# A one-core layer of RWKV-7 and differential attention: the triangle solve by rows down to nine columns, its results stored lane by lane, the x norm placed otherwise, K and V loaded by heads

## The chip, the cores and the metric

The kernel runs on one core of a Trainium2 chip. The metric is the device time of one execution in microseconds (us). Lower is better. Everything is in float32.

## The reference, cut to what matters

One layer is applied to two sequences, one of 512 and one of 2048 tokens (d_model 1024), which the kernel lays one behind the other as 2560 tokens.

```python
u = rmsnorm(h, norm_pre);  proj = u @ w_in
c = centred_conv(proj[..., :1728], conv_w, conv_b)          # r, k, v and three LoRA inputs
# RWKV-7 mixer, 8 heads of 64, in both directions of time; per direction and head:
#   sa    = state @ a_t
#   state = state * w_t + sa b_t^T + v_t k_t^T
#   y_t   = state @ r_t
y_rw = (groupnorm(y_fwd + y_bwd) + bonus) * silu(gate0)
# differential attention, 4 heads, q and k normed, ALiBi slopes:
att  = softmax(s0) - lam * softmax(s1);  o = rmsnorm(att @ v)
y_da = o * silu(gate1)
h = h + concat(y_rw, y_da) @ w_out
out = h + sigmoid(h @ ple_gate_w + b) * rmsnorm(p @ ple_proj)
```

The recurrence of a chunk of 128 tokens is turned into products of matrices. For that a unit lower (or upper) triangular matrix of 64 x 64 has to be inverted for each half of a chunk, each of 8 heads and both directions.

## The kernel before, in words

The work runs in stages, each a `Phase` with tiles and semaphores of its own. A barrier of all engines stands at the end of each, so nothing of one stage lies beside the next. Between stages the data goes through scratch tensors in DRAM. Engines run orders that are written out by hand, and a wait on an engine holds everything behind it on that engine. SP issues nearly all transfers, in program order. In order of time:

1. `conv_phase` (tiles named cv). The rmsnorm of x, the projection to the 1728 convolved columns, the convolution, decays, and the packing of operands for the later stages. There are NT = 20 chunks of 128 tokens, NB = 5 blocks of 512 and NK = 20 units k (a block b and a group g of 128 columns, G = 4). Chunks 0 to 3 are normed at the start. Chunk k + 4 is normed inside unit k: ACT squares (`x_square`, L278) and takes the root (`x_root`, L282), DVE scales the tile (`x_scale`, L403 and L405), TensorE transposes four columns of tiles at a time (`x_turn`, L547), and DVE evicts each such group (`x_evict`, L415). TensorE's own work of a unit is three columns of 32 matmuls (`column`, L561), small products, and the corner blocks of the triangle problem (`corners`, L607). The turn of 1/|kk| is `norms_turn` (L568). On DVE a unit goes: `norm` (L444, L447), `scans` (L453 to L464), `x_scale`, taps (L423, L425), `pack` (L479 to L486), `x_evict` (L415), more taps, and `var` (L440). POOL multiplies the packed operands (L268) beside it. On SP the loads of weights for k and v (L189) stand ahead of the loads of chunks 2 to 4 (L193), and `load(c)` waits until chunk c - 2 has been turned.
2. `rest_phase` (rs). TensorE projects 20 tiles of 128 tokens onto q, k, v and two gates (five units of 16 matmuls of 128 x 512 a tile, L903; four PSUM banks) and turns q and k (L885). ACT evicts and applies tanh, DVE does the norm of q and k (L845 to L854) and the gates (L859). Beside that DVE solves the triangles. For each block of 512 tokens (NJ = 5) the problem of each (direction, head half, group, chunk, half chunk) lies in a lane of its own: `al` holds A, `tt` becomes the inverse, both 64 x 64 a lane. Column k takes two instructions over m x n elements, m = k + 1 and n = 63 - k: a product into `tmp` (L833) and an add into `tt` (L835), each behind the one before. For m <= n, that is up to k = 31, the inner loop runs along a row of n neighbouring elements (the row form). From k = 32 it runs over the m elements of a column of `tt`, 64 elements apart (the column form). A planner (`costs`, `ends`) cuts the 63 columns into 12 slices of about equal cost, and a tile of tokens takes three slices. When a block is solved, ACT writes its transpose into `al` (L789), and SP stores both: 32 transfers a block, each of eight lanes in pieces of 256 bytes (L730, L731). In SP's order they stand behind the stores of a finished tile (L713, L716, L721) and ahead of those of the next. The block's `stored` count also lets `al` be loaded (L709) and `tt` be cleared (L763) two blocks later. The small loads of the identity and the five gain vectors (L738, L740) come behind u, the first weights and A, and both TensorE and DVE wait for them.
3. `unit_phase` (un). 80 units of matrix products. Each loads 5 pieces with SP (L964 to L968), two units ahead.
4. `chain_phase` (ch). Carries the states through the chunks.
5. `attention_phase` (at), once for each sequence (4, then 16 blocks of queries). All of K and all of V are loaded with one transfer each (L1386, L1387) into one semaphore `kv`, and TensorE waits for both before its first scores (L1525). DVE reduces the scores (L1478) with a table of distances that ACT copies (L1415).
6. `output_phase` (fn). The output projection and the gated residual.

## Time and profile before

| | us |
|---|---|
| three timed runs | 4258.77, 4259.48, 4265.96 |
| their median | 4259.48 |
| the profiled execution | 4262.29 |
| its span, first to last instruction | 4260.6 |
| TensorE busy in the span | 3633.9 (85%) |
| VectorE busy | 2541.4 (60%) |
| ScalarE busy | 1433.4 (34%) |
| GpSimd busy | 432.1 (10%) |
| mean granted TensorE clock | 0.932 |
| data moved | 406 MB, 95 GB/s on average |

The busy time of an engine is summed over all stages, which have different limits, so a share of the whole span says little. The profiled execution lies 2.81 us above the median of the timed runs, and 1.7 us of it lie outside its span. DMA shares are the mean over the core's 16 DMA engines. [...]

### The profile page before, as it was taken

How to read it: one execution, taken by the hardware profiler on the slowest of the kernel's cores; microseconds unless marked ns; L12 is line 12 of the kernel's file. 1: busy time of each engine (PE TensorE's matmuls, PEld its weight loads, DVE VectorE, ACT ScalarE, POOL GpSimd, SP SyncE). 2: the span in 40 equal slices, each digit the busy share in tenths (PEclk: the TensorE clock that was granted, in tenths of full speed). 3: DMA queues.
4: the chain of work that ended last, by engine and by line, in shares of the span. 5: the costliest groups of instructions: out<-in, count | busy, mean ns of one | idle time of the engine just before them, and what ended most of it. 6: DMA issues, size and time to landing. Idle time of an engine off the chain costs nothing. (4 is left out here: it accounts for less than half of the span.)

```text
span 4260.6 us, 60699 instructions
## 1 busy us (share of the span) xinstructions
PE 3633.9 (85%) x21081; PEld 2409.1 (57%) x21081; DVE 2541.4 (60%) x4079; ACT 1433.4 (34%) x2572; POOL 432.1 (10%) x702
## 2 busy tenths in 40 slices
PE   6989999598798791599999994359999995999999
PEld 5777777243343340488888884336767763444444
DVE  3565556499999994255555552247777773444443
ACT  3444344122222221122222220036666662223232
POOL 0232334100000000111212110000000000000000
PEclk9999999799899895799999997679999997999999
DMA  3333333512342322344343346720000004222221
GB/s 131 119 126 102 119 114 98 202 67 49 92 101 56 100 54 62 91 127 130 127 130 124 128 131 201 233 101 11 12 15 12 12 10 170 78 78 84 96 78 41
DMA packets 411340, 406.16 MB, mean 95 GB/s; under 512 B 186189, under 2 KB 324121, under 8 KB 410081
## 3 DMA queue, kind: packets, MB, share of 16 engines
q1 hardware_dynamic: 405472, 394.26, 29.4%
q10 hardware_dynamic: 5760, 10.49, 0.6%
q8 instruction: 65, 1.06, 0.1%
q14 instruction: 43, 0.34, 0.0%
HBM read 221.17 MB, written 183.50 MB: 95 GB/s over the span
## 5 line engine op out<-in xcount | busy, mean ns | idle before, releaser
L903 PE MATMUL rs_tm<-rs_w,rs_uT 128*128 128x512 f32 x1600 | 711.1, 606 | 121.5 <-DVE rs_tok_out L859 89.2
L903 PEld LDWEIGHTS rs_tm<-rs_w,rs_uT 128*128 128x128 f32 x1600 | 309.0, 195 | 510.0 <-issue 381.2
L561 PE MATMUL cv_pj<-cv_uT,cv_w 128*128 128x257 f32 (+1 forms) x2240 | 521.4, 392 | 0.8 <-DVEq L420 0.8
L561 PEld LDWEIGHTS cv_pj<-cv_uT,cv_w 128*128 128x128 f32 (+1 forms) x2240 | 425.5, 193 | 83.8 <-issue 10.8
L835 DVE TENSOR_TENSOR rs_tt<-rs_tt,rs_tmp 128x63 f32<-128x63 f32 (+31 forms) x315 | 390.6, 1240 | 10.8
L833 DVE TENSOR_TENSOR rs_tmp<-rs_tt,rs_al 128x63 f32<-128x63 f32 (+31 forms) x315 | 348.3, 1106 | 9.4
L1525 PE MATMUL at_g<-at_kT,at_qz 64*128 64x512 f32 x1088 | 302.1, 632 | 51.0 <-DMA at_v<-scratch_v_tok 46.6
L1478 DVE CUSTOM_DVE_ANT_0 at_sca<-at_g,at_nd 128x1024 f32<-128x1024 f32 (+1 forms) x144 | 167.9, 1166 | 203.7 <-PE at_g L1525 203.2
L1547 PEld LDWEIGHTS at_pb<-at_v,at_attT 128*128 128x128 f32 x2176 | 249.8, 192 | 64.5 <-issue 47.0
L1807 PE MATMUL fn_hb<-fn_wo,fn_mixT 128*128 128x512 f32 x640 | 279.7, 595 | 0.3 <-ACT fn_mixT L1667 0.3
L1807 PE MATMUL fn_gb<-fn_wg,fn_hT 128*128 128x512 f32 x640 | 278.0, 592 | 1.7 <-ACT fn_hT L1667 1.7
L1547 PE MATMUL at_pb<-at_v,at_attT 128*128 128x128 f32 x2176 | 265.1, 279 | 13.0 <-ACT at_attT L1436 13.0
L1078 DVE TENSOR_TENSOR un_su<-un_sc,un_mask 128x448 f32<-128x448 f32 x320 | 185.0, 620 | 152.2 <-PE un_sc L1134 152.2
L1106 DVE SCALAR_TENSOR_TENSOR un_carry_out<-un_ob,un_fp,un_ad 64x192 f32<-64x192 f32 x320 | 119.7, 414 | 175.8 <-PE un_ob L1203 175.8
L1807 PEld LDWEIGHTS fn_hb<-fn_wo,fn_mixT 128*128 128x128 f32 x640 | 120.7, 191 | 145.1 <-issue 145.1
L1807 PEld LDWEIGHTS fn_gb<-fn_wg,fn_hT 128*128 128x128 f32 x640 | 120.0, 190 | 145.4 <-issue 145.4
L1525 PEld LDWEIGHTS at_g<-at_kT,at_qz 64*128 64x128 f32 x1088 | 128.9, 190 | 128.3 <-issue 94.9
L1420 ACT ACTIVATE at_sca<-at_sca,at_nm 128x2048 f32<-128x2048 f32 (+1 forms) x80 | 139.5, 1744 | 166.4 <-DVE at_nm L1483 166.4
L1436 ACT COPY at_attT<-at_tb 128x512 f32<-128x512 f32 x272 | 146.8, 587 | 110.0 <-PE at_tb L1540 110.0
L1131 PE MATMUL un_sc<-un_pk 64*128 64x192 f32 x640 | 97.0, 380 | 101.4 <-DMA un_tf<-scratch_nblk 100.3
L1540 PE MATMUL at_tb<-at_ident,at_sca 128*128 128x128 f32 x1088 | 154.1, 284 | 23.3 <-ACT at_attT L1436 17.4
L1540 PEld LDWEIGHTS at_tb<-at_ident,at_sca 128*128 128x128 f32 x1088 | 115.4, 141 | 103.2 <-DVE at_sca L1493 46.5
(235 smaller groups left out, 5601.2 us busy)
## 6 DMA issues: line engine op xcount, KB each, us to landing
un_pk<-scratch_packs SPq DMA_DIRECT2D x80, 640.0 KB, 4.0
scratch_packs<-cv_pk SPq DMA_DIRECT2D x20, 2048.0 KB, 6.7
scratch_carry<-un_carry_out SPq DMA_DIRECT2D x80, 256.0 KB, 2.1
ch_cb<-scratch_carry SPq DMA_DIRECT2D x40, 512.0 KB, 8.3
scratch_local<-un_local_out SPq DMA_DIRECT2D x80, 192.0 KB, 1.9
cv_x<-in_x_dram SPq DMA_DIRECT2D x20, 512.0 KB, 3.3
scratch_uT<-cv_uT SPq DMA_DIRECT2D x5, 2048.0 KB, 8.0
scratch_ablk<-cv_ab SPq DMA_DIRECT2D x80, 128.0 KB, 2.3
```

The costliest lines, as they stand in the source:

```text
L561: last = nc.tensor.matmul(pj[n % 3][0:r, 0:HALF], w[:, c, m * P:m * P + r], uT[b % 2][:, c, HALF * hf:HALF * hf + HALF], start=(c == 0), s ...
L833: st.step(nc.vector.tensor_tensor(part, column, row, ALU.mult))
L835: last = nc.vector.tensor_tensor(target, target, part, ALU.add)
L903: last = nc.tensor.matmul(tm[n % 4][:, :], uT[b % 2][:, k, half], w[:, k, 512 * u:512 * u + 512], start=(k == 0), stop=(k == KC - 1))
L1078: nc.vector.tensor_tensor(su[par][:, d, h, :], sc[h][:, 0:448], mask[:, d, :], ALU.mult).then_inc(s["sc_evac"], 1)
L1420: nc.scalar.activation(t[:, :], t[:, :], ACT.Exp, bias=nm[:, h % 2, m:m + 1], accum_out=rs[:, h % 2, m:m + 1]).then_inc(s["exp_done"], 1)
L1436: nc.scalar.copy(attT[h % 2][:, 4 * k:4 * k + 4, :].rearrange("p c q -> p (c q)"), tb[(k if NB > 1 else h) % 2][:, :]).then_inc(s["tp_evac ...
L1478: nc.vector.tensor_tensor_reduce(out=scores_of(h, m)[:, k * W:(k + 1) * W], in0=gb[m][:, :], in1=nd[par][:, k * W:(k + 1) * W], scale=SLOP ...
L1525: last = nc.tensor.matmul(gb[m][:, c * 512:(c + 1) * 512], qz[par][rows, h, :], kT[rows, h, at:at + 512], start=True, stop=True)
L1540: last = nc.tensor.transpose(tb[(k if NB > 1 else h) % 2][:, c * P:(c + 1) * P], sc0[h][:, (4 * k + c) * P:(4 * k + c + 1) * P], ident[:, :])
L1547: last = nc.tensor.matmul(pb[h % 2][:, 0:P], attT[h % 2][:, c, :], v[:, c, h * P:(h + 1) * P], start=(c == 0), stop=(c == count - 1))
L1807: last = nc.tensor.matmul(banks[i][:, :], lhsT[:, k, :], w[:, k, i * HALF:(i + 1) * HALF], start=(k == 0), stop=(k == kc - 1))
```

## The change

- **Triangle solve.** The row form is taken for n >= 9, so up to k = 54, and the column form only for the last eight columns. The planner's costs are written anew.
- **Solved triangles.** A lane is stored as a whole row of 16 KB in DRAM: `tblk` and `nblk` get the shape (unit, lane of the unit, 64 x 64), the lanes' order in `ablk` changes so that a unit's lanes lie in order, and a block is stored with 16 transfers of 16 lanes in place of 32 of eight. The units read the same pieces of 256 bytes from the new places. The transpose of the last block is done by DVE in place of ACT, behind the last gate of unit 3 and ahead of the last gate of unit 4 and the last norm.
- **Start of rest_phase.** The identity and gains are loaded first.
- **conv_phase.** On SP the loads of chunks 2 and 3 stand ahead of the weights for k and v, that of chunk 4 behind them. On DVE `x_scale` is the first step of a unit (behind `z_taps`). On TensorE the first turn of a chunk stands ahead of `rates`, in place of ahead of the second column.
- **attention_phase.** K and V are loaded a head at a time, in the order k0, k1, k2, v0, k3, v1, v2, v3, each with a semaphore of its own, for which TensorE waits where it first uses that head.

```diff
@@ -153,7 +153,7 @@
         x_v = x_d.rearrange("(c p) d -> c p d", p=P)
         w_v = w_in.rearrange("(k p) n -> p k n", p=P)
         pk_v = packs[0:G * NB * NQ].rearrange("(g b q) p n -> g b p q n", g=G, q=NQ)
-        ab_v = ablk.rearrange("b (d h g q i) (s t) -> g d h b (i s) q t", d=2, h=2, g=G, q=NQ, i=2, t=64)
+        ab_v = ablk.rearrange("b (d g q h i) (s t) -> g d h b (i s) q t", d=2, h=2, g=G, q=NQ, i=2, t=64)
         Z_AT = 3 * RW_WIDTH
         LAST = LORA
         A, BV, K, RKK = 0, 1, 2, 3
@@ -185,15 +185,15 @@
             sp.dma_start(wup[:, :], w_up[0].rearrange("d r c -> (d r) c")).then_inc(s["lora"], 16)
             sp.dma_start(aup[:, :], a_up[0]).then_inc(s["lora"], 16)
 
-            for name, at in (("w_k", 512), ("w_v", 1024)):
-                sp.dma_start(w[:, :, at:at + 512], w_v[:, :, at:at + 512]).then_inc(s[name], 16)
-
             def load(c):
                 sp.wait_ge(s["xt_ready"], E + 2 * c - 2)
                 sp.dma_start(x[c % 2][:, :], x_v[c]).then_inc(s[f"x_in{c % 2}"], 16)
-            for c in (2, 3, 4):
-                if c < NT:
-                    load(c)
+            load(2)
+            load(3)
+            for name, at in (("w_k", 512), ("w_v", 1024)):
+                sp.dma_start(w[:, :, at:at + 512], w_v[:, :, at:at + 512]).then_inc(s[name], 16)
+            if NT > 4:
+                load(4)
 
             def store_pack(k):
                 b, g = k // G, k % G
@@ -516,12 +516,12 @@
             for k in range(NK + 1):
                 if k < NK and k % G == 0:
                     z_taps(k // G)
+                if k + 4 < NT:
+                    x_scale(E + k + 4, k % 4, x[k % 2])
                 if k:
                     norm(k - 1)
                     scans(k - 1)
                 if k < NK:
-                    if k + 4 < NT:
-                        x_scale(E + k + 4, k % 4, x[k % 2])
                     taps(k, 0)
                 if k:
                     pack(k - 1)
@@ -633,12 +633,12 @@
                     norms_turn(k - 1)
                 if k < NK:
                     logits(k)
-                    if k + 4 < NT:
-                        x_turn(k + 4, 0)
                     column(b, 3 + 3 * g)
                 if k >= 2:
                     corners(k - 2, 0)
                 if k < NK:
+                    if k + 4 < NT:
+                        x_turn(k + 4, 0)
                     rates(k)
                     if k + 4 < NT:
                         x_turn(k + 4, 1)
@@ -656,6 +656,7 @@
     NJ = NT // 4
     G = RW_WIDTH // P
     B = 64
+    SHORT = 9
     O = CONV_COLS
     UNIT_COLS = [O + 512, O + 1024, O + 1536, O, O + 2048]
     with Phase(nc, "rs") as ph:
...
-        def views(t):
-            return t.rearrange("(g b q) (i s) (d h) t -> d h b g (q i) s t", g=G, q=4, i=2, d=2)
-        t_v, n_v = views(tblk), views(nblk)
-
-        costs = [2 * (0.1 + 0.02 * min(k + 1, B - 1 - k) + 0.00105 * (k + 1) * (B - 1 - k)) for k in range(B - 1)]
+        t_v, n_v = (t.rearrange("(g b q) (d l) e -> d b g q l e", g=G, q=4, d=2) for t in (tblk, nblk))
+
+        costs = [m * (max(n, 17) if n >= SHORT else 2 * n) + 160 for m, n in ((k + 1, B - 1 - k) for k in range(B - 1))]
         ends = [0]
         for i in range(12):
             k, goal = ends[-1], sum(costs) * (i + 1) / 12
@@ -705,7 +704,7 @@
 
             def load_a(j):
                 if j >= 2:
-                    sp.wait_ge(s["stored"], 512 * (j - 1))
+                    sp.wait_ge(s["stored"], 256 * (j - 1))
                 sp.dma_start(al[j % 2][:, :, :].rearrange("p s t -> p (s t)"), ablk[j]).then_inc(s[f"al_in{j % 2}"], 16)
 
             def store_tok(t):
@@ -721,23 +720,25 @@
                     sp.dma_start(qk_v[t][i], qk_out[t % 2][:, i, :, :]).then_inc(s[f"qk_stored{t % 2}"], 16)
 
             def store_solved(j):
-                sp.wait_ge(s["turned"], j + 1)
+                if j < NJ - 1:
+                    sp.wait_ge(s["turned"], j + 1)
+                else:
+                    sp.wait_ge(s["turned_last"], 1)
                 for d in range(2):
                     one, two = (tt[j % 2], al[j % 2]) if d == 0 else (al[j % 2], tt[j % 2])
-                    for h in range(2):
-                        for g in range(G):
-                            lanes = slice(64 * d + 32 * h + 8 * g, 64 * d + 32 * h + 8 * g + 8)
-                            sp.dma_start(t_v[d][h][j][g], one[lanes, :, :]).then_inc(s["stored"], 16)
-                            sp.dma_start(n_v[d][h][j][g], two[lanes, :, :]).then_inc(s["stored"], 16)
-
+                    for g in range(G):
+                        lanes = slice(64 * d + 16 * g, 64 * d + 16 * g + 16)
+                        sp.dma_start(t_v[d][j][g], one[lanes, :, :].rearrange("p s t -> p (s t)")).then_inc(s["stored"], 16)
+                        sp.dma_start(n_v[d][j][g], two[lanes, :, :].rearrange("p s t -> p (s t)")).then_inc(s["stored"], 16)
+
+            sp.dma_start(ident[:, :], ident_d).then_inc(s["const"], 16)
+            for i, g in enumerate([q_gain] * 4 + [k_gain]):
+                sp.dma_start(gains[:, i:i + 1], g.rearrange("a m d -> (m d) a"), allow_slow_non_contiguous=True).then_inc(s["const"], 16)
             load_u(0)
             for c in range(5):
                 sp.dma_start(w[:, :, 512 * c:512 * c + 512], w_v[:, :, UNIT_COLS[c]:UNIT_COLS[c] + 512]).then_inc(s[f"w{c}"], 16)
                 if c == 0:
                     load_a(0)
-                    sp.dma_start(ident[:, :], ident_d).then_inc(s["const"], 16)
-                    for i, g in enumerate([q_gain] * 4 + [k_gain]):
-                        sp.dma_start(gains[:, i:i + 1], g.rearrange("a m d -> (m d) a"), allow_slow_non_contiguous=True).then_inc(s["const"], 16)
             for t in range(NT + 2):
                 if t % 2 == 0 and t // 2 + 1 < NT // 2:
                     load_u(t // 2 + 1)
...
@@ -783,7 +784,7 @@
             for t in range(NT + 2):
                 if t >= 2:
                     turned(t - 2)
-                if t % 4 == 0 and 1 <= t // 4 <= NJ:
+                if t % 4 == 0 and 1 <= t // 4 < NJ:
                     j = t // 4 - 1
                     act.wait_ge(s["solved"], j + 1)
                     nc.scalar.copy(al[j % 2][:, :, :], tt[j % 2][:, :, :].rearrange("p j t -> p t j")).then_inc(s["turned"], 1)
@@ -821,7 +822,7 @@
                     dve.wait_ge(s[f"al_in{j % 2}"], 16 * (j // 2) + 16)
                 for k in range(ends[at], ends[at + 1]):
                     m, n = k + 1, B - 1 - k
-                    if m <= n:
+                    if n >= SHORT:
                         part = tmp[:, 0:m * n].rearrange("p (j t) -> p j t", j=m)
                         column, row = T[:, 0:m, k:k + 1].broadcast_to([P, m, n]), A[:, k:k + 1, k + 1:B].broadcast_to([P, m, n])
                         target = T[:, 0:m, k + 1:B]
@@ -871,6 +872,8 @@
                 qk_sums(t)
                 slice_of(t, 2)
                 gate(t, 3)
+            j = NJ - 1
+            nc.vector.tensor_copy(al[j % 2][:, :, :], tt[j % 2][:, :, :].rearrange("p j t -> p t j")).then_inc(s["turned_last"], 1)
             gate(NT - 1, 4)
             qk_norm(NT - 1)
 
...
@@ -964,8 +968,8 @@
                 sp.dma_start(pk[par][:, :], packs[n]).then_inc(s[f"in{par}"], 16)
                 for i in range(2):
                     r = slice(64 * i, 64 * i + 64)
-                    sp.dma_start(tt[par][r, :, 64 * i:64 * i + 64], tblk[n][r]).then_inc(s[f"in{par}"], 16)
-                    sp.dma_start(tf[par][r, :, :], nblk[n][r, 2 * i:2 * i + 2, :]).then_inc(s[f"in{par}"], 16)
+                    sp.dma_start(tt[par][r, :, 64 * i:64 * i + 64], t_v[n][i]).then_inc(s[f"in{par}"], 16)
+                    sp.dma_start(tf[par][r, :, :], n_v[n][i][:, 2 * i:2 * i + 2, :]).then_inc(s[f"in{par}"], 16)
 
             def store(n, par):
                 sp.wait_ge(s["carry_evac"], n * 4 + 12)
@@ -1383,8 +1387,18 @@
             def load_q(n, par):
                 sp.dma_start(qz[par][:, :, :], q_v[n]).then_inc(s[f"q{par}"], 16)
             load_q(0, 0)
-            sp.dma_start(kT[:, :, :], k_v).then_inc(s["kv"], 16)
-            sp.dma_start(v[:, :, :], v_v).then_inc(s["kv"], 16)
+
+            def load_k(h):
+                sp.dma_start(kT[:, h, :], k_v[:, h, :]).then_inc(s[f"k{h}"], 16)
+
+            def load_v(h):
+                sp.dma_start(v[:, :, h * P:(h + 1) * P], v_v[:, :, h * P:(h + 1) * P]).then_inc(s[f"v{h}"], 16)
+            for h in range(3):
+                load_k(h)
+            load_v(0)
+            load_k(3)
+            for h in range(1, HD):
+                load_v(h)
             load_q(1, 1)
 
             def body(n, j, par, more):
@@ -1508,13 +1522,14 @@
             pe.sem_inc(s["tp_ready"], 4 * NB)
             pe.sem_inc(s["pv_ready"], 2)
             pe.wait_ge(s["const"], 32)
-            pe.wait_ge(s["kv"], 32)
 
             def scores(n, j, par, h, ks):
 
                 base = n * (4 * GP) + GP * h
                 if h == 0 and 0 in ks:
                     pe.wait_ge(s[f"q{par}"], j * 16 + 16)
+                if 0 in ks:
+                    pe.wait_ge(s[f"k{h}"], 16)
                 for k in ks:
                     for c in range(W // 512):
                         at = k * W + c * 512
@@ -1543,6 +1558,7 @@
                         scores(*two, range(1, NG))
                     pe.wait_ge(s["tp_evac"], n * (4 * NB) + NB * h + NB + 2)
                     pe.wait_ge(s["pv_evac"], n * 4 + h + 1)
+                    pe.wait_ge(s[f"v{h}"], 16)
                     for c in range(count):
                         last = nc.tensor.matmul(pb[h % 2][:, 0:P], attT[h % 2][:, c, :], v[:, c, h * P:(h + 1) * P], start=(c == 0), stop=(c == count - 1))
                     last.then_inc(s["pv_ready"], 1)
@@ -1871,8 +1887,8 @@
-    tblk = scratch("tblk", (NI, P, 4, 64))
-    nblk = scratch("nblk", (NI, P, 4, 64))
+    tblk = scratch("tblk", (NI, 8, 64 * 64))
+    nblk = scratch("nblk", (NI, 8, 64 * 64))
```

## Rows read from the trace of the kernel before

**Rows 1.** Busy time by stretch (us, count); granted clock, DMA share, GB/s end each line.
```profile
42.00:732.00 690.00, 643.62 (x3858) 514.96 (x3860) 376.29 (x570) 291.85 (x493) 194.74 (x144) 0.96 0.33 109
...
797.00:1643.00 846.00, 724.78 (x1752) 326.20 (x1752) 815.23 (x751) 193.77 (x279) 11.19 (x6) 0.93 0.29 78
...
1736.00:2587.00 851.00, 795.33 (x7760) 665.90 (x7760) 427.85 (x1121) 234.54 (x720) 167.22 (x494) 0.98 0.40 126
```

**Rows 2.** Timeline of PE in the conv stage: start us, us, instructions [idle before <-releaser].
```profile
109.72 7.18 PE L561 MATMUL cv_pj<-cv_uT,cv_w 128*128 128x257 f32 x32
...
138.24 7.18 PE L561 MATMUL cv_pj<-cv_uT,cv_w 128*128 128x257 f32 x32
...
408.40 1.12 PE L547 MATMUL cv_xb<-cv_ident,cv_x 128*128 128x128 f32 x4 [4.52 <-DVE cv_x L405]
...
443.13 1.11 PE L547 MATMUL cv_xb<-cv_ident,cv_x 128*128 128x128 f32 x4 [4.53 <-DVE cv_x L405]
```

**Rows 3.** Waits in the conv stage: us in total, times, longest.
```profile
PE cv_xb L547 <- DVE cv_x L405: 45.9, 11, 4.5
```

**Rows 4.** Timeline of DVE in the conv stage.
```profile
407.59 0.75 DVE L405 TENSOR_SCALAR cv_x<-cv_x,cv_xs 128x1024 f32<-128x1024 f32 x1
...
412.82 0.68 DVE L415 TENSOR_TENSOR cv_uT<-cv_xb,cv_gain 128x512 f32<-128x512 f32 x1
...
433.83 1.67 DVE L453 TENSOR_SCALAR cv_th<-cv_th 128x1024 f32<-128x1024 f32 x1
```

**Rows 5.** Timeline of all engines at the start.
```profile
15.38 26.30 SPq L193 DMA_DIRECT2D cv_x<-in_x_dram  x4
...
30.48 1.06 ACT L278 ACTIVATE cv_junk<-cv_x 128x1024 f32<-128x1024 f32 x1 [14.11 <-DMA cv_x<-in_x_dram]
...
42.24 8.06 PE L561 MATMUL cv_pj<-cv_uT,cv_w 128*128 128x257 f32 x23 [0.80 <-DVEq L420]
```

**Rows 6.** DMA issues of the x chunks: count, KB each, median us to landing.
```profile
cv_x<-in_x_dram SPq DMA_DIRECT2D x20, 512.0 KB, 3.3
```

**Rows 7.** Solve instructions by form: count, busy us, mean ns, idle before.
```profile
L835 DVE TENSOR_TENSOR rs_tt<-rs_tt,rs_tmp 128x1023 f32<-128x1023 f32 x10 | 17.5, 1749 | 0.3
...
L833 DVE TENSOR_TENSOR rs_tmp<-rs_tt,rs_al 128x1023 f32<-128x1023 f32 x10 | 15.7, 1568 | 0.2
...
L835 DVE TENSOR_TENSOR rs_tt<-rs_tt,rs_tmp 128x495 f32<-128x495 f32 x10 | 9.2, 925 | 0.3
...
L835 DVE TENSOR_TENSOR rs_tt<-rs_tt,rs_tmp 128x1024 f32<-128x1024 f32 x5 | 6.1, 1226 | 0.2
```

**Rows 8.** Timeline of PE in the rest stage.
```profile
869.29 34.50 PE L903 MATMUL rs_tm<-rs_w,rs_uT 128*128 128x512 f32 x80
...
904.50 34.50 PE L903 MATMUL rs_tm<-rs_w,rs_uT 128*128 128x512 f32 x80
```

**Rows 9.** Timeline of all engines at the end of the rest stage.
```profile
1642.29 0.27 DVE L835 TENSOR_TENSOR rs_tt<-rs_tt,rs_tmp 128x63 f32<-128x63 f32 x1
...
1642.59 7.19 ACT L789 COPY rs_al<-rs_tt 128x4096 f32<-128x4096 f32 x1 [16.17 <-DVE rs_tt L835]
...
1652.38 0.71 SPq L730 DMA_DIRECT2D scratch_tblk<-rs_tt  x1
...
1736.15 0.36 SPq L959 DMA_DIRECT2D un_ident<-in_ident_dram  x1
```

**Rows 10.** Two stretches of the rest stage, columns as in rows 1.
```profile
785.00:790.00 5.00, 0.00 (x0) 0.00 (x0) 0.00 (x0) 0.00 (x0) 0.00 (x0) 0.50 1.05 391
...
1664.00:1674.00 10.00, 0.00 (x0) 0.00 (x0) 0.00 (x0) 0.00 (x0) 0.00 (x0) 0.50 0.31 55
```

**Rows 11.** Attention: the group of L1525 on the page, then the timeline of the second sequence.
```profile
L1525 PE MATMUL at_g<-at_kT,at_qz 64*128 64x512 f32 x1088 | 302.1, 632 | 51.0 <-DMA at_v<-scratch_v_tok 46.6
...
2843.56 1.90 ACT L1415 COPY at_nd<-at_wide 128x2048 f32<-128x2048 f32 x1 [3.94 <-DVE at_wide L1457]
...
2864.66 1.23 DVE L1478 CUSTOM_DVE_ANT_0 at_sca<-at_g,at_nd 128x1024 f32<-128x1024 f32 x1 [20.88 <-PE at_g L1525]
```

9 lines of the change are left out of this document (5 added, 4 removed).

## The prediction

> **What bounds the kernel now.** I read the stretches first, since stages are closed off by barriers. In the conv stage TensorE is the busy engine, in the rest stage VectorE is (815 of 846 us, TensorE 725), in the unit stage TensorE again, with the DMA engines at 0.40 [rows 1]. So each stage has a bound of its own, and four of them are touched.
>
> Then the idle time of the busy engine. In conv, TensorE waits for the scaled x tile: 45.9 us in 11 waits, nearly all 4.5 us long [rows 3]. A unit with such a wait has a period of 34.73 us (443.13 less 408.40), one with a wait of only 0.66 us had 28.52 (138.24 less 109.72) [rows 2]. The difference is more than the wait: products just after it run slower. On DVE the x tile comes last of a long run of scans, at 407.59 [rows 4].
>
> In rest, a tile of TensorE's work without a stall takes 35.21 us (904.50 less 869.29) [rows 8]; the stage takes (1642.56 - 797)/20 = 42.28 us a tile [rows 1, 9], which is VectorE's. The end of that stage has no product in it: from the end of the solve at 1642.56 to the first instruction of the next stage at 1736.15 are 93.6 us [rows 9], in which eight-lane stores move 55 GB/s [rows 10]. The second attention has its distances ready at 2845.46, yet reduces its first scores at 2864.66, after all of K and V [rows 11].
>
> **The change part by part.** The sum is against the profiled execution, 4262.3 us, which lies 2.8 above the median of the timed runs. A difference of 0.2% (8.5 us) is about what a measurement of this kernel can tell from no change.
>
> *Start of conv.* x chunk 2 is issued at 15.38, behind two weights of 2.1 MB each, and is used at 30.48 [rows 5]. Issued ahead of them it should take the median landing of such a load, 3.3 us [rows 6], so 18.7. From the landing of chunks 2 and 3 to TensorE's first column passed 42.24 - 30.48 = 11.8 us of dependent steps [rows 5]; chunk 3 is now issued when chunk 1 is turned, some 5 us behind chunk 2, and lands while chunk 2 is worked on. First column at 18.7 + 11.8 = 30.5: -12. What is moved past: both weights go 8 us later, to about 21, and land by 33 at 391 GB/s [rows 10]; the key column is wanted near 56, so nothing waits. Chunk 4's load waits behind them, lands near 37, and ScalarE stands before it; its first eviction is due at 37. Three PSUM banks cover that.
>
> *Steady conv.* DVE scales x first, so the tile is ready well before its turn, and the turn moves behind the second column. Ten waits of 4.5 us go, with their slow products: 34.73 less (28.52 - 0.66) is 6.9 each, 69 together. What is late next: (a) x_scale stands ahead of `norm`, whose turn TensorE wants after its first column. POOL runs then, and a DVE pass over 1024 elements takes 1.67 us there in place of 0.75 [rows 4]. The turn of 1/|kk| began near 436.9 (443.13, less the wait of 4.53 and 1.7 us of turn and logits) [rows 2], and it was ready when the next DVE step began at 433.83 [rows 4], so 3 us early. It comes about 2 us later now: cover remains, but only 1 us. (b) x_scale now waits for a second ScalarE root, 0.1 to 0.3 us. (c) `rates` and its 1.1 us are all that cover the eviction between both turns; DVE came to that eviction at 412.82 [rows 4], about when the moved turn would now end, so between 0 and 1.1 us a unit. I take -67, between -55 and -69.
>
> *Solve.* At 1023 elements the mean of ten is 1.749 and 1.568 us, five of each form; the row form at 1024 is 1.226 [rows 7]. So the column form costs 2.27 and 1.91, and a column saves 1.74 us. At 495 elements the add's mean is 0.925 [rows 7]; with a row form of 0.67 (one element in 1.04 ns and the same fixed part as at 1024) its column form is 1.18, and the pair saves 0.81. Over the 23 columns the same reckoning gives 33.4 us a block. The row form at 1024 has 32 rows and shows no charge for them; rows under 31 elements are not in the trace. Bounds: no charge, or the floor of 17 cycles a row that the new planner assumes, which costs 3.95 us a block. VectorE then needs 42.28 - 33.4/4 = 33.9 us a tile, or 34.9. Both are under TensorE's 35.21, so I need not choose: TensorE becomes the bound. 20 x 35.21 = 704 us in place of 845.6. TensorE may start some 8 us earlier, as the gains no longer come behind A, but the five weights are 10.5 MB and still pace the first tile, and u itself goes 3.3 us later behind six small issues; A lands at about 797 as before. I give the start 2 us: -143.5. ScalarE's 7.2 us transposes are covered by four PSUM banks. SP has the stores of a block between those of two tiles. At 55 GB/s a block's 4.19 MB hold it for 76 us [rows 10], over two tiles; at the rate below they are done when the next tile's stores are wanted.
>
> *End of rest.* The transpose leaves ScalarE (7.19 us [rows 9]) for DVE, and ahead of the last gate and norm. DVE's price for 4096 strided elements is not in the trace. It lies between 2.2 us (two elements a cycle) and 8 (the column form's rate [rows 7]); I take 5. Behind it are queued gate, norm, turn, evictions and SP's stores of q and k, 7 us, so the stores start 12 us after the solve, in place of 9.8 [rows 9]: +2. The stores are 4.19 MB. Lower bound: all 16 DMA engines at 391 GB/s, 11 us. Upper bound: the rate is unchanged, 55 GB/s, 76 us [rows 10]. The nearest row is the same store with eight lanes at a time. With 16 a time I take twice the rate, 110 GB/s, 38 us: -38. Landing and barrier gain 1 at most. End of rest: -36 (-63 to +2).
>
> The trace has a share of 0.31 in that stretch, five engines' worth of 16 [rows 10]. [...]
>
> *Units.* They read pieces of 256 bytes as before, from other places; n in twice as many pieces. DMA engines are at 0.40 and loads go two units ahead [rows 1]: nothing, up to 10 us.
>
> *Attention.* Scores start with k0 in place of after 8.4 MB. The second sequence is then bound by its distances: 2864.66 - 2845.46 = -19. The waits for K and V were 46.6 us in both [rows 11]; the first sequence has a quarter of the bytes, so -4. What the new waits hold up: TensorE stands in front of each head's first use, with all its later products behind. Only k0 is used at once; the first product with V comes behind two heads of scores, exponentials and turns. V in pieces of 512 bytes may take longer, but has that cover.
>
> Sum: -12 - 67 - 143.5 - 36 - 19 - 4 = -281.5; 4262.3 - 281.5 = 3981, and 3978 in terms of the median. I say 3980.
>
> **Rivals.**
> - [...] 10%.
> - *Stores over all engines at full rate*, 11 us: 3953. 10%.
> - *TensorE's wait in conv turns into another* (a late 1/|kk| or the eviction between both turns, 4 us in 13 units): about 4025. For it: covers of 1 us. 12%.
> - *Slower than before: short rows are dear.* Place: L833 and L835 for n = 9 to 31. The 23 columns have 1012 rows, twice a block, so each cycle a row costs beyond its elements is 2.1 us a block. VectorE is the bound again from three cycles on. The other parts give 138 us, so the kernel is slower from (138/5 + 33.4)/2.1 = 29 cycles a row; at 35 it would be about 4325. Against: 32 rows of 32 cost nothing [rows 7]. 2%.
> - *The change does less than it says in rest*: something else (the order on SP, gates waiting on tanh) keeps a tile at 38 us: 4035. 8%.
>
> **How the numbers follow.** The forecast has 58%, with a range of its own of 3955 to 4010. The range 3945 to 4060 takes in the second, third and fifth rival and leaves out the first and the slow one, and some of the tails. Faster by over 0.2%: all cases but the dear rows, and a rest for what I don't see: 0.97; same 0.01; slower 0.02.
>
> **What would show it.** In the changed profile: TensorE's first product of conv near 30; no wait of 4.5 us for cv_x, and a period near 28; in rest periods of 35.2 on PE and VectorE idle in front of the gates; L833 and L835 at 1023 elements at 1.22 us both; the transpose on DVE at 2 to 8; stores that take 38 us at 110 GB/s; at_g 19 us earlier. It would be wrong if rest keeps VectorE at 96%, if solve instructions with rows under 17 take more than their elements and the floor, or if SP still stands for 70 us in the stores.

## The result, and the profile after

The changed kernel takes 3978.18 us (median of four runs, 3975.73 to 3979.64), the kernel before 4259.81 on the same footing. The ratio is 0.9338, with a 95% interval of 0.9327 to 0.9349. The forecast was 3980. The profiled execution took 3975.73 us with a span of 3974.0; against the profiled execution of before (span 4260.6) that is 286.6 less.

Since barriers close off the stages, each can be timed from its first instruction to the first of the next:

| stage, us | before | after | difference | forecast |
|---|---|---|---|---|
| conv | 774.4 | 696.6 | -77.8 | -79 |
| rest, up to the end of the solve | 868.1 | 717.3 | -150.8 | -143.5 |
| rest, behind the solve | 93.6 | 53.2 | -40.4 | -36 |
| units | 842.5 | 842.0 | -0.5 | 0 |
| chain | 174.5 | 175.7 | +1.2 | 0 |
| first attention | 80.7 | 78.4 | -2.3 | -4 |
| second attention | 707.5 | 689.2 | -18.3 | -19 |
| output | 719.3 | 721.6 | +2.3 | 0 |

The stretches, which answer to [rows 1] with the same columns (busy time of TensorE, of its weight loads, of VectorE, ScalarE and GpSimd). In all rows below PE is TensorE, DVE is VectorE, ACT is ScalarE, SPq is SP's queue of transfers, and a bracket holds the engine's idle time just before, with what ended it:

```profile
32.00:654.00 622.00, 621.50 (x3854) 497.48 (x3856) 372.92 (x570) 291.94 (x495) 198.14 (x144) 1.00 0.37 123
...
711.00:1414.00 703.00, 701.59 (x1737) 318.38 (x1738) 650.56 (x747) 190.25 (x270) 11.19 (x6) 1.00 0.28 99
...
1467.00:2309.00 842.00, 794.18 (x7760) 664.08 (x7760) 427.26 (x1120) 234.89 (x720) 167.96 (x494) 0.99 0.40 125
```

TensorE is busy for 621.5 of 622 us in conv and 701.6 of 703 in rest, and its granted clock is 1.00, full speed, in both (0.96 and 0.93 before). VectorE fell from 96% of the rest stretch to 93%. The unit stage is as it was.

*Conv.* The timelines of SP and of TensorE at the start, then TensorE in the steady part, to be read beside [rows 5] and [rows 2]:

```profile
16.17 5.47 SPq L190 DMA_DIRECT2D cv_x<-in_x_dram  x2
...
26.45 5.48 SPq L190 DMA_DIRECT2D cv_x<-in_x_dram  x2
...
32.50 23.01 PE L561 MATMUL cv_pj<-cv_uT,cv_w 128*128 128x257 f32 x96 [0.80 <-DVEq L420]
```

```profile
359.73 7.20 PE L561 MATMUL cv_pj<-cv_uT,cv_w 128*128 128x257 f32 x32
...
387.71 7.20 PE L561 MATMUL cv_pj<-cv_uT,cv_w 128*128 128x257 f32 x32
```

x chunk 2 is issued at 16.17 and the first column starts at 32.50 (30.5 was forecast, 42.24 before). The same column of two neighbouring units starts 27.98 us apart; units with a stall had 34.73. No wait for cv_x is left in the steady part.

*Rest, the loop.* Two periods of TensorE, answering to [rows 8], then the solve instructions by form, answering to [rows 7]:

```profile
1312.33 34.50 PE L906 MATMUL rs_tm<-rs_w,rs_uT 128*128 128x512 f32 x80
...
1347.54 34.50 PE L906 MATMUL rs_tm<-rs_w,rs_uT 128*128 128x512 f32 x80
```

```profile
L836 DVE TENSOR_TENSOR rs_tt<-rs_tt,rs_tmp 128x1023 f32<-128x1023 f32 x10 | 12.2, 1225 | 0.3
...
L834 DVE TENSOR_TENSOR rs_tmp<-rs_tt,rs_al 128x1023 f32<-128x1023 f32 x10 | 12.3, 1225 | 0.3
...
L836 DVE TENSOR_TENSOR rs_tt<-rs_tt,rs_tmp 128x495 f32<-128x495 f32 x10 | 6.7, 674 | 0.3
...
L836 DVE TENSOR_TENSOR rs_tt<-rs_tt,rs_tmp 128x448 f32<-128x448 f32 x10 | 8.8, 877 | 0.3
```

The period is 35.21 us, as forecast. Both instructions over 1023 elements are at 1.22 us. Row forms of 1023 elements (1225 ns) and of 448 (625 ns, from a run below) give 1.04 ns an element and 158 ns fixed. By that 495 elements take 674 ns, and they do, though half of that group runs over 55 rows of nine. So rows of nine cost nothing beyond their elements. The group of 448 mixes a row form (eight rows of 56) with a column form (eight columns of 56), and at 877 ns on the mean the latter is 1.13 us where the former is 0.62. Over a block, products and adds together fell from 147.8 to 114.6 us, so by 33.2 (33.4 forecast).

*Rest, its start.* First VectorE before, then the load of A before (its issue, and the time to its landing), then the timeline after:

```profile
797.00 0.34 DVE L864 TENSOR_SCALAR rs_gains<-rs_gains 128x1 f32<-128x1 f32 x4 [48.27 <-DMA rs_gains<-in_da_k_norm_dram]
...
797.26 0.21 DVE L833 TENSOR_TENSOR rs_tmp<-rs_tt,rs_al 128x63 f32<-128x63 f32 x1
...
834.91 0.69 DVE L859 SCALAR_TENSOR_TENSOR rs_tok_out<-rs_tok_out,rs_tm 128x512 f32<-128x512 f32 x1 [3.65 <-ACT rs_tok_out L809]
```

```profile
775.76 1.87 SPq L709 DMA_DIRECT2D rs_al<-scratch_ablk  x1
```

```profile
rs_al<-scratch_ablk SPq DMA_DIRECT2D x1, 2048.0 KB, 15.8
```

```profile
701.52 0.34 DVE L865 TENSOR_SCALAR rs_gains<-rs_gains 128x1 f32<-128x1 f32 x4 [30.69 <-DMA rs_gains<-in_da_k_norm_dram]
...
711.19 9.01 PE L906 MATMUL rs_tm<-rs_w,rs_uT 128*128 128x512 f32 x16 [24.32 <-DMA rs_w<-in_w_in_dram]
...
716.05 0.23 DVE L834 TENSOR_TENSOR rs_tmp<-rs_tt,rs_al 128x63 f32<-128x63 f32 x1 [14.20 <-DMA rs_al<-scratch_ablk]
```

Before, VectorE's first step waited until 797.00, for the gains, as the releaser's name tells. A had landed at 791.6 (775.76 + 15.8), and the solve follows at 797.26 without a wait. The gains' transfers took 12.9 to 16.6 us to land there, behind the large ones, and take 2.1 to 2.4 now. After, they are in at 701.52, TensorE starts with the first weights at 711.19, and VectorE waits for A until 716.05. Counted from the first issue of the stage (774.43 before, 696.58 after), TensorE's first product comes 14.6 us behind it in place of 22.6, and VectorE's first step of the solve 19.5 in place of 22.8.

*Rest, its end*, answering to [rows 9], and a stretch of the stores, answering to [rows 10]:

```profile
1413.91 0.69 DVE L860 SCALAR_TENSOR_TENSOR rs_tok_out<-rs_tok_out,rs_tm 128x512 f32<-128x512 f32 x1
...
1414.51 3.73 DVE L876 COPY rs_al<-rs_tt 128x4096 f32<-128x4096 f32 x1
...
1424.42 0.62 SPq L731 DMA_DIRECT2D scratch_tblk<-rs_tt  x1
...
1443.07 1.29 SPq L732 DMA_DIRECT2D scratch_nblk<-rs_tt  x1
...
1467.10 0.36 SPq L963 DMA_DIRECT2D un_ident<-in_ident_dram  x1
```

```profile
1446.00:1452.00 6.00, 0.00 (x0) 0.00 (x0) 0.00 (x0) 0.00 (x0) 0.00 (x0) 0.50 0.26 109
```

The transpose takes 3.73 us on VectorE (7.19 on ScalarE before, 5 estimated). The 16 stores are issued from 1424.42 to 1443.07, and the next stage starts at 1467.10. From the first of them to the next stage pass 42.7 us (83.8 before, from 1652.38 to 1736.15 [rows 9]). The rate is 109 GB/s at a share of 0.26, which is 4.2 of 16 DMA engines. The target's outer count is four.

*Second attention*, answering to [rows 11]:

```profile
2571.81 3.69 PE L1540 MATMUL at_g<-at_kT,at_qz 64*128 64x512 f32 x8 [12.10 <-DMA at_kT<-scratch_q_kT]
...
2573.08 1.90 ACT L1429 COPY at_nd<-at_wide 128x2048 f32<-128x2048 f32 x1 [3.94 <-DVE at_wide L1471]
...
2575.81 1.23 DVE L1492 CUSTOM_DVE_ANT_0 at_sca<-at_g,at_nd 128x1024 f32<-128x1024 f32 x1 [2.50 <-PE at_g L1540]
```

TensorE's idle time ahead of its first scores is 12.1 us, and K's first head ends it. The table of distances is ready at 2574.98 (2573.08 + 1.90), where it had stood ready for 19 us before. TensorE's eight scores end at 2575.50, and the first reduction follows them at 2575.81. So the distances, the bound that was forecast, are 0.5 us short of binding: the scores, and K ahead of them, still end last.

### The profile page after: what moved, and what is told of

It reads as the page before. It is cut to its first block and busy times, and to the rows that moved or that the text cites. A ratio compares the mean times of both kernels' runs of the same rounds, so it can differ in the third digit from the quotient of the medians.

```text
span 3974.0 us, 60663 instructions
## 1 busy us (share of the span) xinstructions
PE 3594.7 (90%) x21081; PEld 2386.5 (60%) x21081; DVE 2378.0 (60%) x4080; ACT 1426.8 (36%) x2571; POOL 436.5 (11%) x702
## 5 line engine op out<-in xcount | busy, mean ns | idle before, releaser
L906 PE MATMUL rs_tm<-rs_w,rs_uT 128*128 128x512 f32 x1600 | 692.1, 594 | 25.5 <-DMA rs_w<-in_w_in_dram 25.5
L561 PE MATMUL cv_pj<-cv_uT,cv_w 128*128 128x257 f32 (+1 forms) x2240 | 502.9, 382 | 0.8 <-DVEq L420 0.8
L561 PEld LDWEIGHTS cv_pj<-cv_uT,cv_w 128*128 128x128 f32 (+1 forms) x2240 | 410.1, 186 | 90.0 <-issue 22.9
L834 DVE TENSOR_TENSOR rs_tmp<-rs_tt,rs_al 128x63 f32<-128x63 f32 (+31 forms) x315 | 284.1, 902 | 23.6 <-DMA rs_al<-scratch_ablk 14.2
L836 DVE TENSOR_TENSOR rs_tt<-rs_tt,rs_tmp 128x63 f32<-128x63 f32 (+31 forms) x315 | 288.9, 917 | 10.8
L1434 ACT ACTIVATE at_sca<-at_sca,at_nm 128x2048 f32<-128x2048 f32 (+1 forms) x80 | 139.5, 1744 | 143.5 <-DVE at_nm L1497 143.5
L1066 ACT COPY un_local_out<-un_ob 64x256 f32<-64x256 f32 x160 | 58.7, 367 | 321.6 <-PE un_ob L1207 321.6
```

The costliest lines, as they stand in the source:

```text
L561: last = nc.tensor.matmul(pj[n % 3][0:r, 0:HALF], w[:, c, m * P:m * P + r], uT[b % 2][:, c, HALF * hf:HALF * hf + HALF], start=(c == 0), s ...
L834: st.step(nc.vector.tensor_tensor(part, column, row, ALU.mult))
L836: last = nc.vector.tensor_tensor(target, target, part, ALU.add)
L906: last = nc.tensor.matmul(tm[n % 4][:, :], uT[b % 2][:, k, half], w[:, k, 512 * u:512 * u + 512], start=(k == 0), stop=(k == KC - 1))
L1434: nc.scalar.activation(t[:, :], t[:, :], ACT.Exp, bias=nm[:, h % 2, m:m + 1], accum_out=rs[:, h % 2, m:m + 1]).then_inc(s["exp_done"], 1)
```

## The experiments

Every kernel is the changed one with the edit shown. The stage times come from the profile of each run, taken as in the table above.

**The solve alone undone.**

```diff
-                    if n >= SHORT:
+                    if m <= n:
```
(and the old `costs`)

> The changed kernel with the triangle solve as before (row form only for m <= n, column form from k = 32, the old planner); all else as changed. My theory: VectorE bounds the rest stage again, 42.28 us a tile in place of 35.2, so the loop takes 846 to 849 us in place of 703 and the whole about 3978 + 144 = 4122 us (4110 to 4130); TensorE waits again for gates, and its granted clock in that stretch goes back from 1.00 to about 0.93. Rival: a good part of the rest stage's gain came from the early small loads and from the shorter stores on SP, not from the solve: then it is under 4080.

Measured: 4122.67 us (4118.96 to 4125.66), as expected. The rest stage up to the end of the solve is 861.1 us against 717.3. The loop's stretch, then TensorE's waits in it (us in total, times, longest):

```profile
711.00:1557.00 846.00, 725.78 (x1752) 326.52 (x1752) 814.27 (x745) 193.28 (x278) 11.19 (x6) 0.93 0.23 82
```

```profile
PE rs_tm L906 <- DVE rs_tok_out L860: 88.1, 8, 18.9
```

So the solve is worth 144 us, and it is worth that because it brings VectorE's time for a tile under TensorE's. With the old solve the waits for VectorE return, and the clock is at 0.93 again. Those 88 us are not the whole. TensorE's own work on the same 1752 products and turns is 20 us longer at the lower clock (725.8 against 705.6), and the solve ends 32 us behind TensorE's last projection, where in the changed kernel it ends 3 us ahead of it. Together that is the 144. Even with VectorE as the bound, this kernel keeps 7 us of the start's gain (868.1 before, 861.1 here): VectorE's first step of the solve comes 3.3 us sooner, and its wait of 3.65 us for the first tile's gate (834.91, above) is gone.

**The rows down to one element.**

```diff
-                    if n >= SHORT:
...
+                    part = tmp[:, 0:m * n].rearrange("p (j t) -> p j t", j=m)
```
(for all columns, with `costs` = m * n + 152)

> The changed kernel with the row form for all columns, down to rows of one element, and the planner on m*n elements + 152. Theory A (no charge a row, as rows of 9 took 675 ns for 495 elements in the changed kernel): at 63 rows of one element an instruction takes (63 + 152)/0.96 = 224 ns, at 56 rows of eight 625 ns in place of 0.9 to 1.1 us; a block is 3.7 us shorter on VectorE, and the time does not move, since TensorE bounds the loop and the last stores wait for q and k: 3978 within 3. Theory B (a floor of 17 cycles a row): the instruction of 56 rows of eight takes 1.15 us, and time again does not move.

Measured: 3978.19 us (3976.68 to 3980.50). A form in the solve, then the last pair of the last block:

```profile
L829 DVE TENSOR_TENSOR rs_tt<-rs_tt,rs_tmp 128x448 f32<-128x448 f32 x10 | 6.2, 625 | 0.3
```

```profile
1416.28 0.26 DVE L827 TENSOR_TENSOR rs_tmp<-rs_tt,rs_al 128x63 f32<-128x63 f32 x1
...
1416.57 0.27 DVE L829 TENSOR_TENSOR rs_tt<-rs_tt,rs_tmp 128x63 f32<-128x63 f32 x1
```

Eight rows of 56 and 56 rows of eight take the same 625 ns, which is (448 + 152)/0.96: these constants are the 158 ns and the 1.04 ns an element of above. 63 rows of one element take 0.26 and 0.27 us where the elements alone would take 0.22, so there something is added, but some 0.04 us in all. Theory A holds down to rows of eight, and the floor of 17 cycles in the planner, by which the 56 rows of eight would take 1.15 us, describes nothing here. The eight columns that the change leaves in the column form take 10.6 us of a block there and 7.0 here, but VectorE has that time. The solve even ended 3 us later (720.2 us from the stage's start), since the new `costs` begin the last slice at column 53 in place of 56.

**The stores alone undone.**

```diff
+                    for h in range(2):
                         for g in range(G):
-                        lanes = slice(64 * d + 16 * g, 64 * d + 16 * g + 16)
+                            lanes = slice(64 * d + 32 * h + 8 * g, 64 * d + 32 * h + 8 * g + 8)
```
(with the old places in DRAM)

> The changed kernel with the solved triangles stored as before: 32 transfers a block of eight lanes, pieces of 256 bytes, the old order of lanes; all else as changed. My theory: the end of the rest stage goes back to 55 GB/s and is 36 to 40 us longer; inside the loop SP stands 76 us a block but two tiles of 35.2 us hide it: 4016 us (4012 to 4022). Rival: with tiles of 35.2 us in place of 42.3 the stores of the next tiles come late and TensorE waits 7 to 15 us in each of four blocks: 4045 to 4080.

Measured: 4019.62 us (4014.36 to 4050.96). The end of the stage is 95 us in place of 53, +42, and TensorE waits for nothing in the loop but the weights of the first tile, as in the changed kernel. In the stores:

```profile
1440.00:1450.00 10.00, 0.00 (x0) 0.00 (x0) 0.00 (x0) 0.00 (x0) 0.00 (x0) 0.50 0.32 56
```

The rival falls in the profiled execution (4019.34 us). The stores of a block hold SP for 76 us, more than two tiles of 35.2, and in one block the next tile's stores are issued at 1255.91 where the changed kernel issues them at 1206.64, but the buffers cover that. One of the four executions took 4050.96 us, inside the rival's range, at a mean clock of 0.942 where the others have 0.953 and 0.954; no trace shows why.

This run also prices the transpose's move to VectorE, which it keeps: its end of the stage, 94.9 us, is not shorter than the 93.6 before. What made the end shorter is the form of the stores. That form changed in three ways at once: 16 lanes a transfer in place of eight, pieces of 16 KB in place of 256 bytes, and the target's outer count. No run tells whether the old 55 GB/s came from the lanes or from the small pieces.

**Engines or lanes?** The forecast took twice the rate for twice the lanes, an estimate of mine, while the trace shows four engines' worth at work, as many as the target's outer count. The changed kernel's 109 GB/s fits both (twice 55, or four engines at 109/4 = 27), so it can't tell them apart. Three kernels can:

```diff
-    tblk = scratch("tblk", (NI, 8, 64 * 64))
+    tblk = scratch("tblk", (2, NI, 4, 64 * 64))
```
(16 lanes of one store lie in a row in DRAM; a unit reads in seven loads)

> The changed kernel with another place in DRAM for the solved triangles (direction, unit, lane), so that the 16 lanes of one store lie one behind the other there: the outer count of the target is 16 in place of 4. Still 16 transfers of 16 neighbouring lanes a block; the units read with seven loads in place of five. Theory engines: the store was carried by four DMA engines (share 0.26 of 16 at 109 GB/s); now 16 carry it, the end of the rest stage runs at 200 to 390 GB/s and is 17 to 27 us shorter: 3951 to 3961. Theory lanes: 16 neighbouring lanes give 109 GB/s however many engines ask, at a higher share of the engines: 3978 within 3.

```diff
-                    for g in range(G):
-                        lanes = slice(64 * d + 16 * g, 64 * d + 16 * g + 16)
+                    lanes = slice(64 * d, 64 * d + 64)
```
(in addition to the edit above)

> As the run with 16 lanes and outer count 16, but one store takes the 64 lanes of a direction, with four groups as the target's outer count: 4 transfers a block in place of 16, and four engines by the outer count. Theory engines: 109 GB/s as in the changed kernel, 3978 within 3. Theory lanes: four times the lanes give 200 GB/s or more, and the end is 17 us or more shorter: 3961 or less. If both limit, neither run alone is faster.

```diff
-    tblk = scratch("tblk", (NI, 8, 64 * 64))
+    tblk = scratch("tblk", (4, NI, 2, 64 * 64))
```
(64 lanes in one store, in the old order; the direction and the head half are the outer index, so that head half and group make an outer count of 2 x 4 = 8 for one store; five loads a unit. The 27 GB/s an engine are the changed kernel's 109 over four, and 218 is eight times that.)

> The changed kernel with the solved triangles placed in DRAM by (direction, head half, unit, half chunk) and the old order of lanes: one store takes 64 lanes with outer count 8, 4 transfers a block, and a unit still reads with five loads. If an engine carries at most 27 GB/s and the lanes are no limit at 64: 8 engines, 218 GB/s, the end of the rest stage 19 us shorter, unit stage unchanged: 3959 (3956 to 3966). If outer count does not set the engines: as the run with 64 lanes and outer count 4, about +10 on the end: 3988. The unit stage tells in the same run whether the 98 us lost with seven loads came from their number (then it is 842 again) or from the places read (then it is not).

Measured: 4069.72 us (4065.66 to 4077.72), 4083.48 (4080.45 to 4085.69) and 3964.93 (3963.01 to 3967.36). Two stretches of the last stores of each, in this order:

```profile
1436.00:1442.00 6.00, 0.00 (x0) 0.00 (x0) 0.00 (x0) 0.00 (x0) 0.00 (x0) 0.50 0.80 131
...
1442.00:1448.00 6.00, 0.00 (x0) 0.00 (x0) 0.00 (x0) 0.00 (x0) 0.00 (x0) 0.50 1.01 161
```

```profile
1432.00:1440.00 8.00, 0.00 (x0) 0.00 (x0) 0.00 (x0) 0.00 (x0) 0.00 (x0) 0.50 0.26 63
...
1460.00:1470.00 10.00, 0.00 (x0) 0.00 (x0) 0.00 (x0) 0.00 (x0) 0.00 (x0) 0.50 0.25 108
```

```profile
1430.00:1435.00 5.00, 0.00 (x0) 0.00 (x0) 0.00 (x0) 0.00 (x0) 0.00 (x0) 0.50 0.51 118
...
1445.00:1450.00 5.00, 0.00 (x0) 0.00 (x0) 0.00 (x0) 0.00 (x0) 0.00 (x0) 0.50 0.46 174
```

| stores | engines by share | GB/s | end of rest, us |
|---|---|---|---|
| 16 lanes, outer 4 (changed) | 4 | 98 to 109 | 53.2 |
| 16 lanes, outer 16 | 13 to 16 | 131 to 161 | 44.4 |
| 64 lanes, outer 4 | 4 | 63 to 108 | 62.9 |
| 64 lanes, outer 8 | 7 to 8 | 118 to 174 | 42.7 |

The share follows the outer count in each. With four engines, four times the lanes bring no gain, and the same 16 lanes with 16 engines go above 109. So it is the four engines, at up to 27 GB/s each (109 and 108 over four), that bind the changed kernel, and not its lanes. With more engines the rate rises, though far less than in proportion: 15 to 22 GB/s an engine with eight, 8 to 10 with 16 on neighbouring lanes. So neither theory of mine is whole. The 131 to 161 GB/s are also more than the 109 that the theory on lanes leaves to 16 of them, though stores from other lanes were in flight beside them. What holds the runs with eight and with 16 engines below 175 GB/s was not found out, nor why 64 lanes with four engines start at 63 and end 10 us later than 16 lanes do. The third run's time lies in its range (3956 to 3966), but not by its reason: 218 GB/s and an end 19 us shorter were expected, the end is 10.5 us shorter, and 3.6 us came from the unit stage, where nothing was expected.

The first two kernels were 92 and 105 us *slower* in sum, and the place is the unit stage: 940 us in place of 842. The waits of TensorE there, then SP and TensorE around one unit with seven loads, then with five (the changed kernel):

```profile
PE un_sc L1136 <- DMA un_tf<-scratch_nblk: 100.2, 78, 1.8
```

```profile
1908.77 0.35 SPq L968 DMA_DIRECT2D un_pk<-scratch_packs  x1
...
1913.09 0.60 SPq L973 DMA_DIRECT2D un_tf<-scratch_nblk  x1
...
1915.44 0.60 PE L1136 MATMUL un_sc<-un_pk 64*128 64x192 f32 x4 [1.38 <-DMA un_tf<-scratch_nblk]
```

```profile
1911.06 0.35 SPq L968 DMA_DIRECT2D un_pk<-scratch_packs  x1
...
1914.04 0.60 SPq L972 DMA_DIRECT2D un_tf<-scratch_nblk  x1
...
1916.40 0.60 PE L1135 MATMUL un_sc<-un_pk 64*128 64x192 f32 x4
```

SP can issue the first load of a unit only when the unit two before it has given its buffer free. Here that is with a product that ends at 1910.7, so "two units ahead" means 5.7 us ahead of use. With five loads the last is issued 2.98 us later (1914.04 less 1911.06) and TensorE starts at 1916.40, 2.36 us behind that, with no wait in this unit and 5.0 us of waits for n in all. With seven the last is issued 4.32 us behind the first, and TensorE starts 2.35 us behind it (1915.44). It has waited 1.38 us by then, and waits 100.2 us in all units. The last issue comes 1.34 us later than with five, and the wait is 1.38. The run with 64 lanes and outer count 8, which reads other places with five loads, has 838 us. So it is the number of loads, by its time on SP's queue.

**The conv order, each half alone.**

```diff
@@ first kernel, on TensorE @@
+                    if k + 4 < NT:
+                        x_turn(k + 4, 0)
                     column(b, 3 + 3 * g)
@@ second kernel, on VectorE @@
                     scans(k - 1)
+                if k < NK:
+                    if k + 4 < NT:
+                        x_scale(E + k + 4, k % 4, x[k % 2])
```
(each moved back to its old place)

> The changed kernel with TensorE's first turn of a chunk back at its old place, ahead of the second column; DVE still scales x first. Theory A, the scaled tile alone was late and either half of the change cures it: within 3 us of the changed kernel, no wait of 4.5 us. Theory B, the moved turn is what did it: the ten waits of 4.5 us are back, +69 us, 4047. Theory C: the old place covers the eviction between both turns with a whole column, so it is even 1 to 10 us faster.

> The changed kernel with DVE's scaling of x back behind the scans; TensorE's turn stays behind the second column. Theory A, either half is enough: the tile comes 4.5 us behind the old place of the turn, the turn is 8.4 us behind it, so no wait for it, and within 5 us of the changed kernel. Theory B, both are needed: the eviction comes late, behind the tap that follows, and TensorE waits 1 to 4 us in ten units or more: 3990 to 4020. Theory C, the scaling first is what did it: +69 us.

Measured: 3978.18 (3976.78 to 3980.11) and 3976.86 us (3975.28 to 3978.12). Theory A holds in both: either half alone takes all the waits away, and the other adds nothing to the whole. In the first the conv stage is 694.2 us, 2.4 less than in the changed kernel and in the range of theory C, but the unit stage, which it doesn't touch, is 3.9 us longer, so the whole doesn't show it.

**Both halves undone, and K and V whole again.**

> The changed kernel with two stages undone, each behind barriers of its own and read alone: in conv both the scaling of x (behind the scans) and the first turn (ahead of the second column), in attention K and V whole, with one wait. Theory: conv +67 to +69 with ten waits of 4.5 us again, second attention +18 to +20, first +2 to +4: 4066 (4060 to 4072). Rival: the waits come back (45 us) but not the slow products behind them, so conv is only +45 to +50: 4045 to 4052.

Measured: 4071.33 us (4065.60 to 4073.84). Conv is 764.1 us, +67.5; the second attention 709.8, +20.7; the first 82.2, +3.8. The unit stage, untouched, is 847.5, +5.5. TensorE's waits in conv:

```profile
PE cv_xb L547 <- DVE cv_x L405: 45.9, 11, 4.5
```

They are those of [rows 3] to the tenth. So 45.9 us are waits. Of the other 21.6, 20.6 are slower products: the same 4008 products take TensorE 652.7 us here and 632.1 in the changed kernel. The granted clock in the stretch from 400 to 443 us is 0.89 here and before, and 1.00 in the changed kernel. So the rival, waits without slow products, falls.

**Both starts undone.**

```diff
+            for name, at in (("w_k", 512), ("w_v", 1024)):
+                sp.dma_start(w[:, :, at:at + 512], w_v[:, :, at:at + 512]).then_inc(s[name], 16)
             load(2)
             load(3)
-            for name, at in (("w_k", 512), ("w_v", 1024)):
...
-            sp.dma_start(ident[:, :], ident_d).then_inc(s["const"], 16)
...
                 if c == 0:
                     load_a(0)
+                    sp.dma_start(ident[:, :], ident_d).then_inc(s["const"], 16)
```

> The changed kernel with both orders of loads undone: in conv the weights for k and v ahead of x chunks 2 and 3, in the rest stage the identity and the gains behind u, the first weights and A. Conv's first column comes at 42.2 in place of 32.5, +9.7. In the rest stage, theory A (the traces' difference is this move): first product 22.6 us behind the stage's first issue in place of 14.6, and TensorE bounds all that follows, +8: 3996 together. Theory B (as I predicted, 2 us: VectorE and A set the start): +2, so 3990.

Measured: 3992.54 us (3990.87 to 3994.76), which lies between the two theories' 3996 and 3990 and can't choose. The stages can. Conv's first column is at 41.9, +9.4, and the stage is 10.6 us longer. TensorE's first product of the rest stage comes 21.8 us behind the first issue in place of 14.6, and the stage is 6.7 us longer: theory A, with 7 in place of 8.

**Attempts at a better kernel.** Both start from 64 lanes with outer count 8, with the row form for all columns. The first also takes the new `costs` and issues the identity and the gains from ScalarE's queue. In the first, all of the last block is stored ahead of the last gates, q and k; in the second only its untransposed half:

```diff
+                if t == NT:
+                    sp.wait_ge(s["solved"], NJ)
+                    store_part(NJ - 1, tt, False)
```

> The kernel of the run with 64 lanes and outer count 8, and with: row form for all columns; the untransposed half of the last block stored as soon as it is solved and the other half as soon as it is turned, both ahead of the last stores of the gates, q and k; identity and gains issued by ScalarE's queue in place of SP's. Expected: stores 19 us shorter and 10 us earlier, start of the rest stage 3 us earlier: 3978 - 32 = 3946 (3938 to 3956). If the earlier stores only push q and k behind them, 3952 to 3958.

> The kernel of the run with 64 lanes and outer count 8, with the row form for all columns but the slices of the changed kernel's planner, and in the last block the untransposed half stored as soon as it is solved, the stores of the gates, q and k next, the transposed half last. Theory: the tail is set by what eight engines carry (about 150 GB/s); with rows the solve ends 3 us sooner, so 2.1 MB start 13 us earlier, beside work that goes on, and 2.1 MB remain behind q and k: 14 us from about 1424. The end of the rest stage is 12 to 15 us shorter than with 64 lanes and outer count 8 (3965), so 3951 (3947 to 3957). Rival: the early half fills SP's queue, so that the stores of gates, q and k stand as in the run best_of_parts and the gain is under 4 us: 3961 to 3966.

Measured: 3969.02 us (3963.58 to 3970.40) and 3965.51 us (3963.17 to 3967.33, five runs). SP in the first, then in the second:

```profile
1432.30 23.76 SPq L719 DMA_DIRECT2D scratch_q_kT<-rs_qk_out  x4
...
1461.39 0.36 SPq L959 DMA_DIRECT2D un_ident<-in_ident_dram  x1
```

```profile
1411.00 0.62 SPq L725 DMA_DIRECT2D scratch_tblk<-rs_tt  x1
...
1411.67 0.61 SPq L725 DMA_DIRECT2D scratch_nblk<-rs_tt  x1
...
1421.72 12.65 SPq L720 DMA_DIRECT2D scratch_q_kT<-rs_qk_out  x4
...
1434.41 1.60 SPq L725 DMA_DIRECT2D scratch_nblk<-rs_al  x1
```

The first missed both of its forecasts (3946, or 3952 to 3958 if the early stores only pushed q and k behind them). The second missed its own, 3951, and landed in its rival's range. In both, large stores ahead make SP stand at the small ones: 23.76 us at four stores of q and k in the first, 12.65 in the second, so that the transposed half is issued at 1434.41 in place of about 1425. The rest stage as a whole takes 764.4 us in the first, 758.9 in the second, and 760.5 without either trick. The second's solve ends 3.5 us sooner with rows for all columns (714.2 against 717.8 us from the stage's start), and the early half gives 1.9 of that back behind the solve (44.6 against 42.7). Issuing the identity and gains from ScalarE's queue moved TensorE's first product from 14.6 to 14.2 us: the first weights set it. The lowest median is that of the run with 64 lanes and outer count 8, 3964.93 us (3963.01 to 3967.36), 13 less than the changed kernel; neither attempt can be told from it (3963.58 to 3970.40, and 3963.17 to 3967.33).

## Why the prediction was right, point by point

- **Start of conv**, -12: +9.4 when undone. The first column came at 32.50, 2 us later than the 30.5 worked out. Chunk 2 was issued at 16.17, where the sum took 15.38, and was used 3.3 us later, as taken. The rest of the 2 us is that its scaling now queues on VectorE behind the last eviction of chunk 1 (21.32), where before VectorE stood idle at that point.
- **Steady conv**, -67 (-55 to -69): +67.5 when undone, 45.9 of it waits. The reading that products behind a wait run slower, and go with it, is shown: 20.6 us, in a stage whose clock rose from 0.96 to 1.00. The three worries on new waits (1/|kk|, the second root, the eviction between both turns) came to nothing; in the changed kernel TensorE idles 0.5 us in 622. The rival that rested on them fell. Its price was also miscounted: 4 us in 13 units are 52, so 4032 and not 4025.
- **Solve**, 42.28 to 35.21 us a tile: shown by undoing it, 143.8 us. VectorE's saving was 33.2 us a block where 33.4 was worked out. The step that left open whether a floor of 17 cycles exists did not need it; rows of eight and of nine show none (625 and 674 ns for 448 and 495 elements). The dear rows of the slow rival don't exist either.
- **Start of rest**, part of the -143.5: the step "A lands at about 797 as before" failed, and with it "the five weights still pace the first tile". The start was put at 2 us and is 7. A had landed at 791.6 before; what ended the waits of both engines at 797 were the gains, as the rows name them. After its first product TensorE waits for the later weights for 1.2 us in all. Undoing the move cost 6.7 us where TensorE bounds the stage, and the run with the old solve kept 7 where VectorE does (868.1 to 861.1). The rest of the 7.3 us by which this term was too small is the solve, which ends 702.7 us behind TensorE's first product where the sum took all 704 us of the 20 tiles.
- **End of rest**, -36: -40.4. Transpose 3.7 in place of 5, which was between the bounds of 2.2 and 8 (4096 elements at 0.54 ns are 2.2 us, the pace of a VectorE pass in conv before: 427 ns for 512 elements at L483, less the 152 of L399 for one); the stores start 10.5 us behind the solve (12 forecast) and run at 109 GB/s where 110 was taken. From their first issue to the next stage they took 41.1 us less (42.7 in place of 83.8), where the sum gave 38 and at most 1. The rate itself was right by luck: the sum doubled it because the lanes doubled, which no run shows (64 lanes on four engines reach 108), and what sets it is four engines at 27 GB/s each. The first two rivals, one with a far lower rate and one with a far higher, fell.
- **Units**, 0: right in number and wrong in reason. Spare DMA engines (0.40) and loads two units ahead do not hide loads: the last of five lands about when TensorE asks for it (its issue is 2.36 us ahead of the first product, and with seven loads the last one ends a wait 2.35 us after its issue), and two more cost 98 us. Had the new layout needed seven loads, the forecast would have been off by that.
- **Attention**, -19 and -4: -18.3 and -2.3, and +20.7 and +3.8 when undone. The size is right, but the second sequence is still bound by its first scores, which end 0.5 us behind the distances.

The sum fits the profiled execution to 5 us (-286.6 against -281.5), as the two terms of rest were too small by 7.3 and 4.4 us, while conv and both attentions were too large by 1.2, 1.7 and 0.7. The chain and the output, which nothing touches, moved by +1.2 and +2.3 us.

## What to carry to other kernels

Where stages are closed off by barriers, find the busy engine of each. Speeding it up pays only until the next engine's time per tile is reached (here TensorE's 35.2 us). Read the name of what ended each wait at a stage's start and end, since a transfer of 128 small pieces behind large ones can hold a whole stage (here a gain vector, landed in 16.6 us in place of 2.3). Price a store by the outer count of its target as well as by its bytes (here 109 GB/s at four, up to 174 at eight), and a load in a tight loop by its turn on the issuing queue, not by the mean share of the DMA engines (two more loads cost 1.2 us a unit at a share of 0.36). Undo both halves of a double cure alone: here one of the two was enough.
